# A two-block model on one core: weight splits at the release of their slot, the query operand written during the last key chunk, attention scores behind the queries alone, and matrix work moved within an attention head

## What is computed

```
x = x + gate * ((b_gate * causal_conv3(c_gate * u) * silu(z)) @ w_out)    # b_gate, c_gate, u, z = h @ w_in
k, v = split_heads(modulated_norm(x) @ w_kv)                              # 16 heads of 64
q, z = modulated_norm(x) @ w_qz
z_qk = q . k / 8;  beta = sigmoid(z_qk)                                   # stick-breaking attention, causal
a    = beta_k * product over later keys of (1 - beta);  o = a @ v
x = rmsnorm(x + gate * ((o * silu(z)) @ w_out))
# second block
h = rmsnorm(x);  u_pool, q, k, v = h @ w_in
y_pool = grouped mixing of moving averages (windows 2, 4, 8, 16) of u_pool
y_attn = differential attention, 8 heads of 2 x 64, values of 128
x = x + (sigmoid(h @ w_gate) * (y_pool @ w_branch_pool, y_attn @ w_branch_attn), summed) @ w_out
x = x + square(relu(rmsnorm(x) @ w_up)) @ w_down
```

## Time and profile before

| | |
|---|---|
| three runs | 3180.60, 3183.13, 3187.96 us (median 3183.13) |
| profiled execution | 3186.28 us, its span 3184.5 us |
| PE busy | 2857.3 us |
| DVE, ACT, POOL busy | 1244.8, 1130.6, 719.5 us |
| HBM traffic | 236 MB, 74 GB/s over the span |
| mean granted PE clock | 0.96 |

### The profile page before, as it was taken

The page is one execution under the profiler, slowest core; times in us unless marked ns, Lnnn a source line. Parts: engine busy times, 40 slices in busy tenths (PEclk is TensorE's granted clock), DMA queues, the critical chain, the costliest instruction groups (busy, mean ns, idle before and its releaser), DMA issues.

```text
span 3184.5 us, 38040 instructions
## 1 busy us (share of the span) xinstructions
PE 2857.3 (90%) x13672; PEld 2291.2 (72%) x13672; DVE 1244.8 (39%) x1751; ACT 1130.6 (36%) x1585; POOL 719.5 (23%) x387
## 2 busy tenths in 40 slices
PE   5999998988888875969997998988699999999999
PEld 3888886876766764757785666666487788888887
DVE  5544433125566554360002565655532412212121
ACT  3222213225555553233213666666312311212120
POOL 0222221213444432212221111110022122222222
PEclk8999999999999986989998999999899999999999
DMA  4333322442211120202231000001231111111112
GB/s 194 129 122 119 112 73 73 162 154 73 86 47 52 51 81 27 79 20 86 92 132 56 34 27 33 27 33 47 100 131 46 40 47 53 46 46 53 46 46 99
DMA packets 62570, 236.80 MB, mean 74 GB/s; under 512 B 6945, under 2 KB 7585, under 8 KB 59937
## 3 DMA queue, kind: packets, MB, share of 16 engines
q1 hardware_dynamic: 62496, 235.88, 21.4%
HBM read 191.81 MB, written 44.04 MB: 74 GB/s over the span
## 4 chain that ended last, share of the span: by engine, by line
issue 53%; PE 35%; POOL 5%; DVE 4%; ACT 2%; DMA 0%; POOLq 0%; DVEq 0%; ACTq 0%; SPq 0%
PE PS L542 28%; POOL WL L1795 5%; PE PS L700 2%; PE PS L722 2%; DVE ATL L1372 2%; DVE bC L1550 2%; ACT PS L1095 1%; PE PS L685 1%; PE PS L748 1%; POOL dBIAS L1850 1%; PE PS L705 0%; ACT bB L1094 0%; ACT ATH L1087 0%; PE PS L629 0%; PE PS L823 0%
## 5 line engine op out<-in xcount | busy, mean ns | idle before, releaser
L1795 POOL TENSOR_TENSOR WL<-WR,WH 128x1024 fp32r<-128x1024 f32 x215 | 520.7, 2422 | 2134.3 <-ACT WH L977 2128.3
L542 PE MATMUL PS<-HH,WH 128*128 128x512 f32 x2272 | 729.6, 403 | 122.7 <-issue 38.0
L542 PE MATMUL PS<-HL,WH 128*128 128x512 f32 x2272 | 715.0, 396 | 0.0
L542 PE MATMUL PS<-HH,WL 128*128 128x512 f32 x2272 | 713.1, 396 | 0.0
L542 PEld LDWEIGHTS PS<-HH,WH 128*128 128x128 f32 x2272 | 428.1, 193 | 228.8 <-issue 95.1
L542 PEld LDWEIGHTS PS<-HL,WH 128*128 128x128 f32 x2272 | 436.5, 192 | 94.2
L542 PEld LDWEIGHTS PS<-HH,WL 128*128 128x128 f32 x2272 | 435.7, 192 | 93.4
L977 ACT ACTIVATE WH<-WR 128x1024 fp32r<-128x1024 f32 x214 | 225.6, 1054 | 542.6 <-PE PS L542 366.9
L542 PE MATMUL PS<-GH,WH 128*128 128x512 f32 x768 | 236.6, 389 | 1.5 <-DVE TMP L1765 1.5
L542 PE MATMUL PS<-GL,WH 128*128 128x512 f32 x768 | 236.5, 389 | 0.0
L542 PE MATMUL PS<-GH,WL 128*128 128x512 f32 x768 | 236.4, 389 | 0.0
(11 more groups left out here) (226 smaller groups left out, 3496.6 us busy)
## 6 DMA issues: line engine op xcount, KB each, us to landing
WR<-wst SPq DMA_DIRECT2D x215, 512.0 KB, 3.5
TMP<-mods SPq DMA_DIRECT2D x48, 512.0 KB, 3.6
MRAW<-mods SPq DMA_DIRECT2D x16, 512.0 KB, 10.9
v_hl<-VS SPq DMA_DIRECT2D x8, 1024.0 KB, 6.3
bV<-v_hl SPq DMA_DIRECT2D x8, 1024.0 KB, 7.7
X<-xt SPq DMA_DIRECT2D x4, 1024.0 KB, 9.0
x_b<-X SPq DMA_DIRECT2D x8, 512.0 KB, 4.9
k_hi<-KSH SPq DMA_DIRECT2D x8, 512.0 KB, 4.8
```

The source lines that it names most:

```text
L542: last = pe.matmul(PS[:, dst0 + q:dst0 + q + HALF], l, rr[:, k * S + q:k * S + q + HALF], start=a, stop=z)
L1795: pool.tensor_tensor(WL[slot][:, :], WR0[:, :], WH[slot][:, :].bitcast(F32), ALU.subtract).then_inc(w_lo, 1)
```

## The change

Six edits. (1) `B_FILL`: for the blocks t = 5, 6, 7 matmuls are moved from behind the second turn to ahead of it. (2) The scores of a new head wait for the two query evictions only (`4 * j - 2`); the wait for the gate evictions stays in `steps` ahead of the first matmul of the next fill. (3) The last key chunk is taken out of the loop; PE signals each of its steps through the new `kv_read`, and ACT and DVE write the query operand behind it, with the eviction of the last keys in the midst of it. (4) In the pool and gate stages ACT splits the weights of chunk c+2 as soon as chunk c is done, before it evicts; in the output stage it does so before it writes `GH`. SP issues the weight load ahead of the loads of `g_a` and `m_p`, and the next one at the end of each round. (5) PE waits for `d_st` after the first chunk of the second attention, not before it.

```
-          (7, 5, 0, 0), (10, 6, 0, 0), (6, 2, 0, 4), (14, 6, 0, 0))
+          (7, 5, 0, 0), (9, 3, 0, 0), (10, 2, 0, 4), (18, 2, 0, 0))
...
+            load_w(C_AB + 2)                                  # SP
             sp.wait_ge(f_lo, FILL["ab"] + KT)
             for n in range(KT):
                 if n >= 2:
                     sp.wait_ge(g_lo, KT + n - 1)
                 sp.dma_start(T[n % 2], g_a[n]).then_inc(ab_ld[n % 2], 16)
                 sp.dma_start(T[2 + n % 2], m_p[n]).then_inc(ab_ld[n % 2], 16)
-                load_w(C_AB + 2 + n)
+                if n < KT - 1:
+                    load_w(C_AB + 3 + n)
...
-            with pe.Fori(1, KT) as i:                         # PE
+            with pe.Fori(1, KT - 1) as i:
                 kv_chunks(i)
+            kv_chunks(KT - 1, final=True)   # its key steps signal kv_read
...
-                    pe.wait_ge(b_df, 4 * j)
+                    pe.wait_ge(b_df, 4 * j - 2)
...
-            pe.wait_ge(d_st, 16)
             for n in range(3):
                 chunk(C_QKV2 + n, (C_QKV2 + n) % 2, 0, ud[0] + n)
+                if n == 0:
+                    pe.wait_ge(d_st, 16)
...
+            def last_keys_hi(k):                              # ACT
+                if k == 3:
+                    keys_hi(KT - 1)
+                if k < KT - 1:
+                    act.wait_ge(kv_read, k + 1)
+            fill_hi("qz", 5 * KT, before=last_keys_hi)
...
-                if g:
-                    split_w(c + 1, (c + 1) % 2)
                 act.wait_ge(chunk_done, c + 2)
+                split_w(c + 2, c % 2)
                 act.activation(TP, PAIR[c % 2], ACT.Identity).then_inc(free[c % 2], 1)
...
-                    split_w(2 * i + (C_GA + m + 1), 1 - s)
                     act.wait_ge(chunk_done, 2 * i + (C_GA + m + 2))
+                    split_w(2 * i + (C_GA + m + 2), s)
...
+            split_w(C_AB + 1, (C_AB + 1) % 2)
             for n in range(KT):
                 c = C_AB + n
-                split_w(c + 1, (c + 1) % 2)
+                if n < KT - 1:
+                    act.wait_ge(chunk_done, c + 2)
+                    split_w(c + 2, c % 2)
                 act.wait_ge(ab_m, n + 1)
...
-            fill_lo("qz", 2, lambda k: col(COEF, 2 * KT + k), 5 * KT)              # DVE
+            values_lo(KT - 1)
+            fill_lo("qz", ..., before=lambda k: keys_lo(KT - 1) if k == 4 else None)
```

More of the change, by code:

```diff
@@ L320, in block_kernel @@
         kv_kh = sem("kv_kh")
+        kv_read = sem("kv_read")
         kv_vh = sem("kv_vh")
@@ L544, in mm3, with step @@
                 return last
-            def step(c, slot, pair, RH, RL, k, nk=KT):
+            def step(c, slot, pair, RH, RL, k, nk=KT, read=None):
                 if k == 0:
@@ L554, in step @@
                     last.then_inc(chunk_done, 1)
+                elif read is not None:
+                    last.then_inc(read, 1)
             def chunk(c, slot, pair, used, RH=HH, RL=HL, nk=KT, operand=None):
@@ L622, in _, with kv_chunks @@
             u = USED["kv"]
-            def kv_chunks(i, first=False):
+            def kv_chunks(i, first=False, final=False):
                 def turn_values():
@@ L639, in kv_chunks @@
                             turn_values()
-                        step(2 * i + (C_KV + 1), 1, 1, HH, HL, k)
+                        step(2 * i + (C_KV + 1), 1, 1, HH, HL, k, read=kv_read if final else None)
             kv_chunks(0, first=True)
-            with pe.Fori(1, KT) as i:
+            with pe.Fori(1, KT - 1) as i:
                 kv_chunks(i)
+            kv_chunks(KT - 1, final=True)
             def value_sum(t, n, VH, VL):
@@ L982, in root, with fill_hi @@
                 act.activation(dst, tmp, ACT.Exp, scale=-0.5).then_inc(rs, 1)
-            def fill_hi(name, shift=None):
+            def fill_hi(name, shift=None, before=None):
                 for k in range(KT):
+                    if before:
+                        before(k)
                     act.wait_ge(ftmp, SCALED[name] + k + 1)
@@ L1056, in _, with values_hi @@
             fill_hi("kv", 3 * KT)
-            with act.Fori(0, KT) as i:
+            def values_hi(i):
                 act.wait_ge(chunk_done, 2 * i + (C_KV + 2))
@@ L1063, in _, with keys_hi @@
                 act.activation(value_part(0), PAIR[2].rearrange("p (a d) -> p a d", d=HD), ACT.Identity).then_inc(kv_vh, 1)
+            def keys_hi(i):
                 act.wait_ge(chunk_done, 2 * i + (C_KV + 3))
@@ L1067, in _ @@
                 split_w(2 * i + (C_KV + 3), 1)
-            fill_hi("qz", 5 * KT)
+            with act.Fori(0, KT - 1) as i:
+                values_hi(i)
+                keys_hi(i)
+            values_hi(KT - 1)
+            def last_keys_hi(k):
[4 more added lines that the diff above has]
+            fill_hi("qz", 5 * KT, before=last_keys_hi)
             act.wait_ge(f_lo, FILL["qz"] + KT)
@@ L1184, in _ @@
                     s = (C_GA + m) % 2
-                    split_w(2 * i + (C_GA + m + 1), 1 - s)
                     act.wait_ge(chunk_done, 2 * i + (C_GA + m + 2))
+                    split_w(2 * i + (C_GA + m + 2), s)
                     act.activation(T[2], PAIR[s], ACT.Sigmoid, bias=vec("b_gate", 2 * i + (8 + m))).then_inc(free[s], 1)
                     act.wait_ge(ga_st, 32 * i + 16 * (m + 1))
-            split_w(C_GRP + 1, (C_GRP + 1) % 2)
             for g in range(4):
@@ L1505, in _, with values_lo, keys_lo @@
             fill_lo("kv", 2, lambda k: col(COEF, KT + k), 3 * KT)
-            with dve.Fori(0, KT) as i:
+            def values_lo(i):
                 dve.wait_ge(kv_vh, i + 1)
                 low(value_part(1), PAIR[2].rearrange("p (a d) -> p a d", d=HD), value_part(0)).then_inc(free[2], 1)
+            def keys_lo(i):
                 dve.wait_ge(kv_kh, i + 1)
                 low(KSL[:, :], PAIR[1], KSH[:, :]).then_inc(free[1], 1)
-            fill_lo("qz", 2, lambda k: col(COEF, 2 * KT + k), 5 * KT)
+            with dve.Fori(0, KT - 1) as i:
+                values_lo(i)
+                keys_lo(i)
+            values_lo(KT - 1)
+            fill_lo("qz", 2, lambda k: col(COEF, 2 * KT + k), 5 * KT, before=lambda k: keys_lo(KT - 1) if k == 4 else None)
             dve.wait_ge(f_lo, FILL["qz"] + KT)
```

## The result

The changed kernel takes 3134.87 us (median of 4 runs, 3131.19 to 3137.24), the kernel before 3185.55 us in runs beside it (4 runs, 3180.60 to 3193.56): a ratio of 0.9833, 95% interval 0.9818 to 0.9849. The forecast was 3130, the range 3122 to 3143. Its profiled execution takes 3134.09 us, 52.2 less than the profiled one before (3132.9 was predicted for it); the last row of PE ends 52.0 earlier.

The account below looks back on a forecast made before the run. PE, busy 90% of the span, was taken as the bound, with its waits and the low clock behind them as the gain. Five places summed to 53.35 us, from 3186.28 to 3132.9 profiled, 3130 as median; range 3122 to 3143.

Parts of the forecast that it names:

- The last step, from the profile to the median: Whole kernel: the median of the runs was taken as 3.15 us below the profiled execution, 3132.9 to 3130.
- Pool and gate: Pool and gate stages: earlier splits end PE's waits of 8.53 and 2.29 us and two low clock stretches, 14.6 us.
- the same lead: Pool and gate: the 7.4 us by which splits are ready early also hides ACT's evictions coming 1.06 us later.
- Second attention: First chunk starts 8.4 us earlier without waiting for constants, and 4.35 us of low clock goes: 12.75 us.
- Last keys: Last keys and queries: the 8.19 us idle goes, a wait of 2.3 to 2.8 remains inside query chunks: 6.8 us.
- Heads: Seven head boundaries: 1.55 us each from the query wait, 0.2 from the table, 1.4 in all from clock: 13.7 us.
- Output stage: Third chunk's weights: 4.6 us of the 6.70 us wait and half of a 1.9 us low stretch gained: 5.5 us.
- (a): Third pool chunk: DVE's chain locks POOL out until it ends; 3135 us; chance 0.17.
- (b): Heads: scans set the pace, so boundary gains are waited for again in blocks 5 to 7; 3144 us; chance 0.12.
- (d): Output stage: the weight load lands no earlier, so the edit does nothing; 3135.5 us; chance 0.07.
- (e): Output stage: g_a and m_p loads stuck behind a weight load make it slower; eating 53 us needs 25 us landings; chance 0.01.
- (c): Keys, output stage, heads, constants: low clock returns behind the shorter waits; 3135 us; chance 0.12.

Follow-up runs that it names:

- e4: Kernel before with only the wait for the constants of the second attention moved behind its first chunk: 3177.46 us, ratio 0.9968.
- e1: Kernel before with only the scores of a new head waiting for the two query evictions, not the gate's too: 3178.55 us, ratio 0.9963.
- e6: Kernel before with only the two output-stage edits, the split ahead of GH and the weight load ahead of g_a and m_p: 3180.05 us, ratio 0.9985.
- e7: Kernel before with only ACT's half of the output edit, the split ahead of GH, load order as before: 3184.32 us, ratio 0.9995.
- e9: Kernel before with both edits of the heads, the query wait and the B_FILL table, and nothing else: 3171.88 us, ratio 0.9949.
- e3: Kernel before with only the query operand written behind the steps of the last key chunk: 3182.55 us, ratio 0.9986.
- e5: Kernel before with only the splits of the pool and gate stages moved to the release of their slot: 3172.28 us, ratio 0.9960.
- e8: Changed kernel with further reordering at the last keys, the end of the gate stage and the output stage: 3126.94 us, 0.9817 of the kernel before.
- e2: Kernel before with only the new B_FILL table: 3193.82 us, ratio 1.0021.
- e10: Changed kernel with further reordering at the end of the gate stage and the output stage, not the last keys: 3124.88 us, 0.9805 of the kernel before.

## Why the prediction was right

The mechanism held at all five places, and the sum of the measured places, 52.5, is close to 53.35. That the total came so near is in part luck: the heads gave 3.4 us more than predicted and the second attention 2.7 less, and of what had no term, 4.2 us gained ahead of the changed places and at a wait stand against 4.25 lost behind the heads. The last step, from the profile to the median, didn't hold: 3.15 us were taken off, but the changed kernel's median is 0.8 above its profiled execution. That is most of the difference between 3130 and 3134.87.

**Pool and gate, 14.6.** Measured 14.63. POOL gets in between DVE's instructions, as I took it, and the chunks behind the removed waits run at full clock. One thing was missed and cost nothing: I let "the same lead" cover all of ACT's evictions, but the grouped chunks are short, and the second needs the pair of the last gate at once. It waits 1.02 us, and the third, which has waited for YPL all along, waits 3.77 in place of 4.76.

**Second attention, 12.75.** Measured 10.0, the one term that is clearly too high. The wait fell by 8.38, as worked out. The 4.35 for the low stretch was mis-sized: "with no wait of 9.7 ahead I count it as gained". In the changed kernel 2.7 of it came back around waits of 2.12 and 1.20: 17.26 us from the first chunk's start to the second's and 18.22 from there to the third's, where 16.41 is the length at full clock. In e4, with 16.44 and 17.97, 1.6 came back.

**Last keys, 6.8.** Measured 6.35, with the wait of 2.55 inside the interleaved chunks in the range of 2.3 to 2.8, and the low stretch behind it.

**Heads, 13.7.** Measured 17.1 in seven heads, or 17.8 with the seventh boundary, whose wait fell from 1.90 to 1.27. The step gave 1.55 a boundary, counting from the fill; in e1 the fill does start only 1.6 us earlier (1.83 us behind the scores, at 1086.93, where the earlier trace rows have 1.55), but the head is 1.9 shorter: the chain of scores, scans and turns, which moves by the full 1.91 of the wait, sets its length, not the fill. The table's 0.2 is right. "I count half" for the clock of every second head was too little: it ended in all of them, 0.8 us in three heads, and 0.7 us more of low clock ended in the first head. So of the 17.8 about 12.8 are the query wait (as in e1; 10.85 predicted), 3.2 clock (1.4 predicted), and the remaining 1.8 the table (1.4 predicted). The last head then lost 4.2 us with the stage behind it, which no step had.

**Output stage, 5.5.** Measured 4.3: 4.5 for the wait and none of the low stretch.

**The rivals.** Shown wrong: (a) by POOL's rows, (b) by e1, (d) by e6 and e7, (e) by the output stage, where no wait above 0.3 us stands ahead of the fourth to eighth chunk. (c), low stretches behind shorter waits, was true at the keys, at the constants and in the output stage, and false in the heads.

**Do the gains add?** By medians e9 16.4, e3 4.6, e4 9.7, e5 14.4 and e6 6.6 make 51.7; the change gave 50.7 in its first runs and 53.3 in the second. Each of the five has an interval of 3 to 5 us to either side, so this shows only that nothing of 10 us or more is missing. Within that they add, apart from the two edits of the heads (-8.6 and +6.7 apart, -16.4 together), whose difference is a low stretch that one wait or the other keeps alive.

## What to carry to other kernels

Judge two edits of one loop together: an edit that only moves a wait can cost time alone and give time beside the edit that removes the wait where it moves to. Read each stage's length and granted clock, not the total, and take a second profile of the same kernel before an effect of some us in an untouched stage is believed or explained. Before work on POOL is moved earlier, look up which DVE instruction is issued just then and who stands behind it in DVE's order.

## What the runs showed of the hardware

- DVE and POOL take turns at their shared access: a POOL split that came second waited 0.5 us (changed kernel) and 1.1 us (e5), less than one of DVE's eight back-to-back instructions (1.21 us), and DVE's next one then took 3.4 us for 1.28; in e8 a DVE instruction that came 0.16 us after POOL took 3.39 us for 1.28.
- The clock of TensorE fell to its lower level (1.2 GHz) behind waits of 2.25 us between busy stretches in every second head (both profiles of before, e4 to e7) or in three of six (e1), in e3 also behind 2.18, behind 3.1 in all of six heads (e2), and, where no wait is above 1.35, in one head of thirty (the heads 2 to 7 in two profiles of the changed kernel, e8, e9 and e10; the one is in e8).
- Where the low stretches fall was the same in two executions of one kernel over 1200 us, and different in kernels whose code there is the same but which arrive otherwise: the heads of e3 (+5.4 us), the second attention of e4, e5 and e7 (+6.3 to +6.4) and e6 (-2.8). What decides it stays open; no run here changes the moment of arrival alone.
